# Forward sweep of a bidirectional state-space scan: masks of both directions first, 64-row products in alternating row halves, backward output added by an identity product

## The reference, cut to what matters

```python
acs = jnp.cumsum((dt * a)..., axis=2)                 # within a chunk
decay = jnp.exp(jnp.where(lower, acs_t - acs_s, -inf))  # one 128x128 matrix for each head
cb = jnp.einsum('bctgn,bcsgn->bctsg', cc, bc)         # one 128x128 matrix for each group
y_diag = jnp.einsum('bctsgr,bcsgrp->bctgrp', cb[..., None] * decay, xdt)
y_off = jnp.einsum('bctgn,bcgrpn,bctgr->bctgrp', cc, s_in, jnp.exp(acs))
y = y_f + rev(y_b)                                    # both directions
```

## Time and profile before

| | us |
|---|---|
| median of 3 runs | 2864.4 (2863.81 to 2864.73) |
| the profiled execution | 2862.88 |
| its span in the trace | 2861.1 |
| busy: PE / DVE / ACT / POOL | 2707.4 / 1666.9 / 609.7 / 983.4 |
| the eight passes of the forward sweep | 1765.5 to 1870.1, some 105 |

### The profile page before, as it was taken

How to read it: one execution, slowest core, us unless ns; L and a number is a source line. 1 busy time by engine, 2 the same in 40 slices (tenths; PEclk the granted TensorE clock), 3 DMA queues, 4 the chain that set the end, 5 groups by cost and what they waited for, 6 DMA issues and landing times. The chain is left out here.

```text
span 2861.1 us, 32418 instructions
## 1 busy us (share of the span) xinstructions
PE 2707.4 (95%) x12452; PEld 2167.2 (76%) x12452; DVE 1666.9 (58%) x2225; ACT 609.7 (21%) x902; POOL 983.4 (34%) x515
## 2 busy tenths in 40 slices
PE   7899999999999999997888999989989999999997
PEld 5688877778888888865676776568767888888885
DVE  8877545756556665686746985963375222222247
ACT  4232232311110011132332103722131110001111
POOL 2122225553333333451212332013545333333343
PEclk9899999999999999998899999999999999999998
DMA  3111132323222322232001343241332111111123
GB/s 138 38 51 44 50 136 83 99 81 102 90 88 88 103 95 82 95 96 75 26 30 41 101 124 121 100 177 44 110 96 85 52 48 44 51 44 51 44 74 103
DMA packets 88484, 228.88 MB, mean 80 GB/s; under 512 B 27520, under 2 KB 30720, under 8 KB 88384
## 3 DMA queue, kind: packets, MB, share of 16 engines
q1 hardware_dynamic: 52384, 172.81, 18.5%
q10 hardware_dynamic: 36000, 54.69, 6.1%
HBM read 197.98 MB, written 28.31 MB: 79 GB/s over the span
## 5 line engine op out<-in xcount | busy, mean ns | idle before, releaser
L195 POOL CAST w_hi<-w_raw 128x1024 fp32r<-128x1024 f32 x254 | 281.8, 1109 | 1813.0 <-PE ps L208 1801.9
L204 PE MATMUL ps<-a_hi,w_hi 128*128 128x512 f32 x2080 | 693.1, 401 | 47.4 <-POOL w_lo L197 18.4
L197 POOL TENSOR_TENSOR w_lo<-w_raw,w_hi 128x1024 fp32r<-128x1024 f32 x254 | 698.7, 2751 | 20.3
L206 PE MATMUL ps<-a_lo,w_hi 128*128 128x512 f32 x2080 | 676.8, 393 | 0.0
L208 PE MATMUL ps<-a_hi,w_lo 128*128 128x512 f32 x2080 | 674.2, 392 | 0.0
L204 PEld LDWEIGHTS ps<-a_hi,w_hi 128*128 128x128 f32 x2080 | 390.3, 191 | 141.4 <-issue 32.7
L206 PEld LDWEIGHTS ps<-a_lo,w_hi 128*128 128x128 f32 x2080 | 395.2, 190 | 83.5
L208 PEld LDWEIGHTS ps<-a_hi,w_lo 128*128 128x128 f32 x2080 | 393.9, 189 | 84.5
L206 PE MATMUL ps<-g_b,w_hi 128*128 128x512 f32 x1216 | 419.2, 396 | 0.0
L204 PE MATMUL ps<-g_b,w_hi 128*128 128x512 f32 x1088 | 369.7, 397 | 9.9 <-DVE g_b L1770 9.9
L208 PE MATMUL ps<-g_b,w_lo 128*128 128x512 f32 x1088 | 368.5, 396 | 0.0
(11 more groups left out here) (451 smaller groups left out, 2748.4 us busy)
## 6 DMA issues: line engine op xcount, KB each, us to landing
w_raw<-in_wstream SPq DMA_DIRECT2D x254, 512.0 KB, 3.5
ada_w<-in_ada_w ACTq DMA_DIRECT2D x25, 512.0 KB, 3.5
ada_w_m<-in_ada_w ACTq DMA_DIRECT2D x25, 512.0 KB, 3.4
y_by_token<-y ACTq DMA_DIRECT2D x12, 512.0 KB, 3.1
x_res_b<-in_xT SPq DMA_DIRECT2D x2, 2048.0 KB, 11.6
x_block<-x_res_b SPq DMA_DIRECT2D x16, 256.0 KB, 3.7
z_rows<-ada_w ACTq DMA_DIRECT2D x8, 512.0 KB, 2.7
u_rows<-pad ACTq DMA_DIRECT2D x8, 512.0 KB, 4.2
```

The source lines that it names most:

```text
L195: pool.tensor_copy(k.w_hi[:, s, :], k.w_raw[:, s, :]).then_inc(k.w_high, 1)
L197: pool.tensor_tensor(k.w_lo[:, s, :], k.w_raw[:, s, :], k.w_hi[:, s, :].bitcast(F32), ALU.subtract).then_inc(k.w_split, 1)
L204: pe.matmul(o, w_hi, a_hi[:, c], start=first, stop=False)
L206: pe.matmul(o, w_hi, a_lo[:, c], start=False, stop=False)
```

## The change

- `exponents` is split by group. For one group all four mask products come first (both directions, banks 0 to 3), and then the four 64-row products, with the row halves alternating: rows 0 to 63, rows 64 to 127, and again. Both directions of a group so end nearly together.
- `forward(i)` lays the diagonal products between them: exponents of group 0, heads 0 to 5, exponents of group 1, heads 6 to 9, `cb`, heads 10 to 15. The waits for `fore_ready` and for the loaded backward output (`y_in`) now stand behind the exponents of group 0.
- The backward output is no longer added on DVE. For each group PE multiplies it by the identity (float32, 512 columns) and opens with it the accumulation that the diagonal products then add to. DVE's L2669 goes, and `last_sum` adds `fore_tmp` instead.
- ACT's list and the rest of DVE's list stay as they are.

```diff
--- before.py
+++ after.py
@@ -2332,7 +2332,7 @@
         y_of = [y_even[:, :], y_odd]
         ctx_values = [xw, y_even, big[:, 2, :], xw]
         stage = k.ada_w
-        s = signals(nc, ctx, "p5", "chain xw_ready moving_ready d_done e_ready e_sum w_ready cb_done cb_ready off_done fore_ready fore_added "
+        s = signals(nc, ctx, "p5", "chain xw_ready moving_ready d_done e_ready e_sum w_ready cb_done cb_ready off_done fore_ready "
                                    "st_done state_ready diag_done y_ready y_back y_out0 y_out1 y_in0 y_in1 z_out d_out "
                                    "d_in dhi dlo x_done x_free0 x_free1 cleared area_in pooled")
         x_free = [s["x_free0"], s["x_free1"]]
@@ -2419,23 +2419,27 @@
             def here(i):
                 return slice(i * P, (i + 1) * P)
 
-            def exponents(i):
-
-                pe.wait_ge(s["moving_ready"], i + 1)
-                for j in range(EXPS):
-                    g, r, use = j // 2, j % 2, EXPS * i + j
+            def exponents(i, g):
+
+                if g == 0:
+                    pe.wait_ge(s["moving_ready"], i + 1)
+                    if i:
+                        pe.wait_ge(s["cb_ready"], i)
+                banks = [k.ps[:, m, :].rearrange("p (h t) -> p h t", t=P) for m in range(4)]
+                for r in range(2):
+                    use = EXPS * i + 2 * g + r
                     if use >= 2:
                         pe.wait_ge(s["e_ready"], use - 1)
-                    if i and j == 0:
-                        pe.wait_ge(s["cb_ready"], i)
-                    rows = slice(r * P // 2, (r + 1) * P // 2)
-                    outs = [k.ps[:, 2 * r + b, :].rearrange("p (h t) -> p h t", t=P) for b in range(2)]
-                    for out in outs:
-                        pe.matmul(out, ident_r, bc(masks[r], 1, HPG // 2), start=True, stop=False)
-                    for b, out in enumerate(outs):
-                        at = g * HPG + b * HPG // 2
-                        ins = pe.matmul(out, v.l_rows[rows, here(i)], moving[rows, at:at + HPG // 2, :], start=False, stop=True)
-                    ins.then_inc(s["d_done"], 1)
+                    for b in range(2):
+                        pe.matmul(banks[2 * r + b], ident_r, bc(masks[r], 1, HPG // 2), start=True, stop=False)
+                for b in range(2):
+                    at = g * HPG + b * HPG // 2
+                    for r in range(2):
+                        rows = slice(r * P // 2, (r + 1) * P // 2)
+                        ins = pe.matmul(banks[2 * r + b], v.l_rows[rows, here(i)], moving[rows, at:at + HPG // 2, :],
+                                        start=False, stop=True)
+                        if b == 1:
+                            ins.then_inc(s["d_done"], 1)
 
             def products_cb(i):
                 pe.wait_ge(s["e_ready"], EXPS * i + 3)
@@ -2456,21 +2460,33 @@
                 for g in range(NGRP):
                     ins = pe.matmul(X[st_at][:, g, :], v.tok[:, i, g * P:(g + 1) * P], xw[:, half_of(g)], start=True, stop=True)
                 ins.then_inc(s["st_done"], 1)
+                def diagonal(h0, h1):
+                    for h in range(h0, h1):
+                        g, cols = h // HPG, slice(h % HPG * P, (h % HPG + 1) * P)
+                        if h % HPG == 0:
+                            pe.matmul(X[y_at][:, g, :], k.mats[:, IDENT, :], y_of[i % 2][:, half_of(g)], start=True, stop=False)
+                            pe.wait_ge(s["w_ready"], 2 * i + g + 1)
+                        ins = pe.matmul(Xf[y_at][:, h * HDIM:(h + 1) * HDIM], weights[g][:, cols],
+                                        v.tok[:, i, VAL + h * HDIM:VAL + (h + 1) * HDIM], start=False,
+                                        stop=h % HPG == HPG - 1)
+                    return ins
+
                 if i + 1 < NC:
-                    exponents(i + 1)
+                    exponents(i + 1, 0)
+                pe.wait_ge(s["fore_ready"], i + 1)
+                pe.wait_ge(y_in[i % 2], 16 * (i // 2 + 1))
+                diagonal(0, 6)
+                if i + 1 < NC:
+                    exponents(i + 1, 1)
+                diagonal(6, 10)
+                if i + 1 < NC:
                     products_cb(i + 1)
-                pe.wait_ge(s["fore_ready"], i + 1)
-                for h in range(SSM_HEADS):
-                    g, cols = h // HPG, slice(h % HPG * P, (h % HPG + 1) * P)
-                    if h % HPG == 0:
-                        pe.wait_ge(s["w_ready"], 2 * i + g + 1)
-                    ins = pe.matmul(Xf[y_at][:, h * HDIM:(h + 1) * HDIM], weights[g][:, cols],
-                                    v.tok[:, i, VAL + h * HDIM:VAL + (h + 1) * HDIM], start=True, stop=True)
-                ins.then_inc(s["diag_done"], 1)
+                diagonal(10, SSM_HEADS).then_inc(s["diag_done"], 1)
 
             for q in range(2):
                 pe.wait_ge(k.pair_free[q], UZ_END // 2)
-            exponents(0)
+            for g in range(NGRP):
+                exponents(0, g)
             products_cb(0)
             for q in range(2):
                 pe.wait_ge(x_free[q], fwd // 2)
@@ -2643,8 +2659,8 @@
 
             def last_sum(i):
                 dve.wait_ge(s["diag_done"], i + 1)
-                dve.wait_ge(s["fore_added"], i + 1)
-                tt(y_of[i % 2], y_of[i % 2], Xf[(i + 1) % 2], ALU.add).then_inc(s["y_ready"], 1)
+                dve.wait_ge(s["fore_ready"], i + 1)
+                tt(y_of[i % 2], fore_tmp, Xf[(i + 1) % 2], ALU.add).then_inc(s["y_ready"], 1)
                 if i < SPLIT_EARLY:
                     dve.wait_ge(s["dhi"], i + 1)
                     tt(v.a_lo[:, i, :], stage[:, :], v.a_hi[:, i, :].bitcast(F32), ALU.subtract).then_inc(s["dlo"], 1)
@@ -2664,9 +2680,6 @@
                 else:
                     dve.wait_ge(s["d_out"], 16 * KT)
                 tt(heads(fore_tmp), heads(Xf[(i + 1) % 2]), per_head(v.e_acs, i, 0), ALU.mult).then_inc(s["fore_ready"], 1)
-                dve.wait_ge(y_in[i % 2], 16 * (i // 2 + 1))
-                dve.wait_ge(s["fore_ready"], i + 1)
-                tt(y_of[i % 2], y_of[i % 2], fore_tmp, ALU.add).then_inc(s["fore_added"], 1)
                 dve.wait_ge(s["st_done"], i + 1)
                 dve.wait_ge(s["state_ready"], i + 1)
                 ch.link(tt(heads(state[:, :]), heads(state[:, :]), per_head(v.e_tot, i, 0), ALU.mult))
```

## The result

The changed kernel takes 2908.5 us (2906.3 to 2910.5, 4 runs) against 2864.1 for the kernel before (2861.8 to 2864.7, 4 runs). The ratio is 1.0162, with a 95% interval of 1.0148 to 1.0176. The forecast was 2892 with a range of 2876 to 2900: the sign was right, the size was too small, and the time lies outside the range.

What follows compares the result with a forecast made beforehand. The prediction took a loop through ACT and DVE (`moving`, `a_hi`, `a_lo`) to set every other pass. Passes summed to +20.3 and the clock to +7.5, together +27.8, giving 2890.7; the median's 1.5 offset led to 2892, range 2876 to 2900.

Steps and rivals of the forecast that it cites:

- What bounds the kernel now: Sweep before the change: a loop through ACT and DVE (`cb`, `moving`, `a_hi`, `a_lo`, weights) sets every other pass, 13.22.
- The loop after the change: Passes 1 to 5, `cb` to `cb`: 17.15 against 13.47 a pass, 3.68 more each, +18.4 in five.
- I take 1.5 each time ... five times: +7.5; bounds 0 and 3: Passes 1 to 5: PE's pause of 3.8 before the first identity product lowers the granted clock, costing 1.5 us each.
- two of the three pauses shown left the clock alone: Support for the holding-clock rival: the clock stayed full after pauses of 1.97 and 2.54, not after 3.73.
- Masks, changes and 64-row products: One group's exponents on PE: masks 0.90, two tiling changes 0.43, four products side by side 0.45, together 1.78.
- Pass 0: First pass of the sweep: `moving` 0.9 later as masks wait for the second exponential; the pass ends 0.85 later.
- Passes 6 and 7: Last two passes: pass 6 takes 13.32 against 13.84, -0.5; pass 7 takes 9.95 against 8.44, +1.5.
- The loads hidden, DVE's addition worth nothing: Loads of `y_in` and the pooled tile cost nothing; removing L2669, off the loop, gains nothing.
- The clock did not hold: Rival, passes 1 to 5: same loop but the clock stays full, +20, 2884.5; chance 0.20.
- the products did not fall apart: Rival, 64-row products: they don't overlap or load weights openly, 0.45 more a group, +4, 2896; chance 0.08.
- PE's own work became the bound: Rival, not slower: PE bounds at 12.79 a pass if `a_lo` doesn't wait for `a_hi`, 2862.3; chance 0.12.

Runs made afterwards that it cites:

- before_late_low: The kernel before with only `a_lo` of the previous pass moved behind DVE's addition L2669; 2859.7 us, ratio 0.9994.
- fill_two: The changed kernel with PE's pause filled by repeating the two state products twice behind group 0's exponents; 2893.1 us, ratio 1.0112.
- late_low: The changed kernel with DVE doing the previous pass's `a_lo` behind `fore_tmp` instead of behind `last_sum`; 2866.1 us, ratio 1.0018.
- between_only: The kernel before with only the diagonal products laid between the two groups' exponents and `cb`, old exponents, addition on DVE; 2897.7 us, ratio 1.0131.
- masks_only: The kernel before with only the new form of the exponents, both groups in the old place; 2887.1 us, ratio 1.0073.
- halves_apart: late_low with the 64-row products not alternating, two of one row half and then two of the other; 2867.3 us, ratio 1.0015.
- all_mended: late_low with `moving` made in two halves, chunk 0's exponents in the old form, and DVE's addition for the last chunk; 2857.4 us, ratio 0.9985.
- masks_filled: masks_only with one state product repeated behind each group's exponents, filling its two pauses of 1.11; 2882.9 us, ratio 1.0083.

## Why the prediction was right or wrong

- **What bounds the kernel now: right.** The loop through `moving`, `a_hi` and `a_lo` set the passes; before_late_low evened them to 12.76. That is PE's own pass there, which I had put at 13.0 in what I expected of that run.
- **The loop after the change: right.** 17.15 was forecast, and fill_two shows 17.20 at the full clock. From `cb` to the identity product it was 11.42, where 11.45 was forecast. late_low and between_only show that it is the order, and the wait for `a_hi` in front of the weights, that made it.
- **"I take 1.5 each time ... five times: +7.5; bounds 0 and 3": wrong, and this is the step that failed.** The clock's cost per pass was mis-sized. The changed kernel's five passes are 19.8 longer than fill_two's, 4.0 each, above even my upper bound of 3. So the passes took 19.2 to 23.9, where I had put 17 to 19. I sized it from products of 512 columns behind a pause, where the half clock lasted under 4 us. Here other work stands behind the pause, and it lasted 7 to 17 us. heads_wide, with wider head products and nothing else changed, gets the full clock back sooner and takes 8.8 less in the five passes, so the work behind the pause is a part of it; what makes the rest stays open. I also read a row too shortly. I wrote that the clock stayed full after the pause of 2.54. It did in the first 5 us, but in the next 5, behind two more pauses of 0.80 and 1.17 around transposes of 128 columns, it was 0.66:

```profile
1910.00:1915.00 5.00, 3.60 (x16) 2.97 (x16) 5.00 (x6) 2.12 (x2) 0.00 (x0) 0.66 0.01 2
```

So "two of the three pauses shown left the clock alone" was no safe ground either: the pause of 2.21 in pass 2 and those of 1.11 in masks_only were followed by the half clock.

- **Masks, changes and 64-row products: right in size.** A group was put at 1.78 and takes 1.12 + 0.67 = 1.79. That the alternation is what brings it, as I expected of halves_apart, is refuted. The Trainium skill ("TensorEngine Tiling (Array Packing)", Key Properties) says that different tiles can execute in parallel. The traces agree: two products in one half took 0.67 with the change, and four in both halves took 0.67.
- **Pass 0: too small.** I put `moving` 0.9 later and nothing for the clock. The sweep's start has pauses of 1.11, 0.20 and 1.11, which I had costed as delays only, and behind them the clock fell before the first off product (its two products take 3.33 instead of 1.72). It came to +1.8 instead of +0.85. In all_mended, with the old form of the exponents at the start, pass 0 has the full clock.
- **Passes 6 and 7: right.** They came out at -0.48 and +1.75, where -0.5 and +1.5 were forecast. The terms given for pass 7 add up to 9.92 and not 9.95, which changes nothing.
- **The loads hidden, DVE's addition worth nothing: right.** PE never waits for `y_in`, and the loss is there with and without the addition.
- **The rest of the span.** 1.9 ahead of the sweep and 3.1 behind it were not forecast. Of the 3.1, the load of `z_rows` that holds the chain takes 26.34 instead of 25.03. No run here was made to explain the rest; behind the sweep the clock falls at other places in the two traces.
- **The rivals.** The clock did not hold, and the products did not fall apart. PE's own work became the bound in all_mended, at 12.74 a pass where 12.79 was put: there `a_lo` no longer stands in front of `fore_tmp`, which is the condition that the forecast had named, and `moving` comes in two halves as well.

## What to carry to other kernels

When a wait is moved forward on one engine, list what the instruction it waits for has in front of it on its own engine: here PE's diagonal came to hang on a DVE list in which an unrelated rounding stood first. A pause of PE must be priced with all the work that stands behind it at half speed, and how long that lasts is better read from a place in the trace with the same kind of work behind the pause, and given a wide range: here it was 7 to 17 us in one kernel. If an order leaves several short pauses, look at the granted clock even if none of them is long.

## What the runs showed of the hardware that I had not expected

- Four 64-row products in two halves of the rows took 0.67 with the change of shape, the same as two products in one half with the change, and the same in either order.
- In pass 1 of the changed kernel, behind a pause of 3.74, the granted clock was 0.51, 0.50 and 0.50 in three stretches of 5 us, with PE busy from the pause's end.
- 28 records of one column in place of the pause (3.3 to 4.3 us) did not hold the clock: ratio 1.0208, against 1.0112 with 8 records of 512 columns in the same place.
- Pauses of 1.11, 0.20 and 1.11 within 5.3 us were followed by the half clock in three of six passes of masks_only. With products in the two longer ones, in masks_filled, it stayed full in all six (15.22 or 15.23 each), at the cost of 1.4 us a pass against masks_only at the full clock.
